# Key products of 64 tokens in two column groups, and waits and placements moved in attention and DeltaNet

## The reference

```
h  = rms_norm(x)*(1+scale)+shift            # scale, shift, gates from silu(c) @ ada_w
p  = h @ w_in                               # q/kv latents, q,k,v of DeltaNet, z, a, b, pooling
attention: 4 heads, softmax(q k^T) v        # latents see all 768 keys, context its own 256
DeltaNet, both directions, 4 heads of 128:  # q, k, v = silu(conv3(.)), q and k normalised
   g = -exp(a_log)*softplus(a+dt), beta = sigmoid(b), gc = cumsum(g) in the chunk
   T = I + strict_lower(beta k k^T * exp(gc_i-gc_j));  w, u = T^-1 (beta k exp(gc)), T^-1 (beta v)
   S <- S exp(gl) + kd^T (u - w S);   o = qg S + (q k^T * decay)(u - w S)
out = [attention, rms_norm(o)*silu(z), pooling] @ w_out;  x += gate1*out
x += gate2*expert_choice_moe(h2)            # 16 experts, top tokens, SwiGLU
```

## Time and profile before

| | us |
|---|---|
| median of 3 runs | 1804.51 (1804.24 to 1807.38) |
| profiled execution | 1800.79 |
| its span, first to last instruction | 1798.7 |
| attention of layer 0, and its DeltaNet tiles | from about 249, from 382 |
| attention of layer 1, and its DeltaNet tiles | from about 1218, from 1308 |
| TensorE's mean granted clock | 0.979 of 2.4 GHz |

### The profile page before, as it was taken

How to read it: one execution, slowest core, us unless ns; L and a number is a source line. 1 busy time by engine, 2 the same in 40 slices (tenths; PEclk the granted TensorE clock), 3 DMA queues, 4 the chain that set the end, 5 groups by cost and what they waited for, 6 DMA issues and landing times. The chain is left out here.

```text
span 1798.7 us, 34350 instructions
## 1 busy us (share of the span) xinstructions
PE 1691.2 (94%) x14201; PEld 1036.1 (58%) x14201; DVE 657.7 (37%) x1330; ACT 448.8 (25%) x991; POOL 414.8 (23%) x556
## 2 busy tenths in 40 slices
PE   6999989879999997999999999999978999999998
PEld 4565555547776554555556445555567844454544
DVE  4045233425554152111211425424446634322323
ACT  4211423252433040011111231143353223001010
POOL 2712105025660003111111141301537700000000
PEclk9999999989999998999999999999989999999999
DMA  9520010067875217999998512000121033699996
GB/s 320 152 87 24 1 37 12 4 196 222 267 248 181 70 64 252 371 369 370 368 357 318 166 47 70 24 1 17 57 82 25 14 117 138 264 411 414 406 413 240
DMA packets 160222, 323.53 MB, mean 180 GB/s; under 512 B 30217, under 2 KB 117999, under 8 KB 144751
## 3 DMA queue, kind: packets, MB, share of 16 engines
q1 hardware_dynamic: 127584, 287.20, 42.8%
q0 software_dynamic: 6880, 21.67, 4.5%
q10 hardware_dynamic: 25646, 13.08, 2.7%
HBM read 307.24 MB, written 14.68 MB: 179 GB/s over the span
## 5 line engine op out<-in xcount | busy, mean ns | idle before, releaser
L676 PE MATMUL psum<-hT,ring 128*128 128x512 f32 (+3 forms) x880 | 298.7, 497 | 0.0
L676 PEld LDWEIGHTS psum<-hT,ring 128*128 128x128 f32 (+1 forms) x880 | 165.6, 190 | 121.3 <-issue 110.9
L1238 PE MATMUL psum<-ring,arena 128*64 128x256 f32 x1536 | 174.4, 384 | 5.6 <-DVE xT L2633 3.4
L1238 PEld LDWEIGHTS psum<-ring,arena 128*64 128x64 f32 x1536 | 109.0, 138 | 68.2 <-issue 13.4
L1138 PE MATMUL psum<-hT,ring 128*128 128x512 f32 (+1 forms) x384 | 139.4, 521 | 0.9 <-DVE xT L2517 0.9
L2604 DVE TENSOR_TENSOR arena<-arena,psum 128x384 f32<-128x384 f32 (+1 forms) x32 | 15.6, 488 | 258.7 <-PE psum L1247 159.5
L1138 PEld LDWEIGHTS psum<-hT,ring 128*128 128x128 f32 x384 | 72.7, 190 | 64.8 <-issue 61.5
L2977 POOL DMA_INDIRECT big<-h_rows_lat,idx x16 | 15.7, 983 | 377.0 <-PE psum L1343 173.7
L2633 DVE SCALAR_TENSOR_TENSOR xT<-psum,modraw,xT 128x512 f32<-128x512 f32 (+1 forms) x136 | 79.7, 621 | 18.7 <-PE psum L1319 12.7
L808 PE MATMUL psum<-hT,ring 128*128 128x256 f32 (+1 forms) x192 | 83.5, 545 | 0.0
L2042 ACT COPY arena<-psum 128x512 f32<-128x512 f32 (+2 forms) x49 | 23.6, 481 | 220.4 <-PE psum L1260 147.2
(11 more groups left out here) (377 smaller groups left out, 3097.0 us busy)
## 6 DMA issues: line engine op xcount, KB each, us to landing
ring<-in_moe_w_gate SPq DMA_DIRECT2D x64, 1024.0 KB, 10.1
ring<-in_ada_w SPq DMA_DIRECT2D x48, 1024.0 KB, 6.8
ring<-in_moe_w_up SPq DMA_DIRECT2D x32, 1024.0 KB, 9.7
hT<-in_moe_w_down SPq DMA_DIRECT2D x24, 1024.0 KB
ring<-in_w_in SPq DMA_DIRECT2D x20, 1024.0 KB, 7.3
big<-in_moe_w_up SPq DMA_DIRECT2D x16, 1024.0 KB, 10.0
sz<-in_moe_w_down SPq DMA_DIRECT2D x16, 1024.0 KB
big<-in_moe_w_down SPq DMA_DIRECT2D x16, 1024.0 KB
```

Source lines behind the costliest of these rows:

```text
L676: m = pe.matmul(b[0:c1 - c0, 0:n], lhsT=w[:, k, c0:c1], rhs=hT[:, k, t0:t0 + n], start=k == 0, stop=k == KD - 1)
L1238: m = pe.matmul(b[e * CAP_L:(e + 1) * CAP_L, 0:2 * P], lhsT=xs[:, k, e, 0:CAP_L], rhs=w[e][:, 2 * (k - ks[0]) + q, :], start=k == 0, stop= ...
```

## The change

The keys' small products become 64 tokens by 64 in two column groups: 16 matmuls to a bank, in three banks, claimed in calls 0, 1 and 2 and not two in call 1. VectorE multiplies each bank (512 columns) by the mask of the diagonal blocks of 16 and sums over the four column blocks with a reduction, behind its copy of the transposes in those calls. ScalarE stores them in call 3, not 2.

The other placements are given for layer 0 and layer 1. The gates' logarithms: call 2 and 1, not 0. The decays from them: call 4 and 2, not 1. The sums over the decays: call 6 and 3, not 2. Their transpose: call 8 and 4, not 3. The lanes' exponentials: call 11 and 7, not 7. Loading the inverse blocks: call 16 and 12, not 21 and 13. The first tile's kk products: one call earlier. The eight SiLUs and both table loads stand ahead of the copy that sets `att`, and `next_decays` of tile 1 in slots 3 and 5 as in the other tiles. In layer 0's first tile the slots have 0, 1, 0, 1, 1, 1, 2 modulation products. `next_decays` waits for the key transposes of tile j - 2 and for decay_state of that tile, and no longer for its state product. GpSimd makes `masks` ahead of `one_sided`, and before tile 0 `spread` ahead of `masks`, in layer 0 ahead of `decays` too.

```diff
-LANES_EXP = 7
+GATES, SUMS, ROWS, LANES_EXP = (2, 1), (6, 3), (8, 4), (11, 7)
+ADA_SLOTS = ((0, 1, 0, 1, 1, 1, 2), (1, 1, 1, 1, 1, 1, 0))
@@ TensorE, block_lanes
-                    if n == 1:
+                    if n in (0, 1, 2):
                         pe.wait_ge(s["lmul"], GH)
-                        for w in range(2):
-                            b = claim(("pk", l, w))
-                            for x in range(NT * GH // 2):
-                                i, h = divmod(w * NT * GH // 2 + x, GH)
-                                for q in range(4):
-                                    t = slice(i * P + 32 * q, i * P + 32 * (q + 1))
-                                    m = pe.matmul(b[32 * q:32 * (q + 1), 32 * x:32 * (x + 1)], lhsT=qkvT[:, GH + h, t],
-                                                  rhs=qkvT[:, GH + h, t], start=True, stop=True)
-                            done(m, ("pk", l, w))
-                    if n == 2:
+                        b = claim(("pk", l, n))
+                        for x in range(2 * GH):
+                            i, h = 2 * n + x // GH, x % GH
+                            for q in range(2):
+                                t = slice(i * P + HALF * q, i * P + HALF * (q + 1))
+                                m = pe.matmul(b[HALF * q:HALF * (q + 1), HALF * x:HALF * (x + 1)], lhsT=qkvT[:, GH + h, t],
+                                              rhs=qkvT[:, GH + h, t], start=True, stop=True)
+                        done(m, ("pk", l, n))
+                    if n == SUMS[l]:
@@ TensorE, first_chunk
-                    if n in (5, 6):
-                        gdn_piece("kk", 0, n - 5)
+                    if n in (4, 5):
+                        gdn_piece("kk", 0, n - 4)
@@ ScalarE, next_decays
                     if j >= 2:
                         act.wait_ge(s["eb"], 2 * (j - 2) + d + 1)
-                        evacuated(act, ("st", l, j - 2, d))
+                        evacuated(act, ("kr", l, j - 2, d))
+                    if j >= 3:
+                        act.wait_ge(s["sdec"], 2 * (j - 3) + d + 1)
@@ ScalarE, gdn_between
-                    if j == 0 and slot < 4:
-                        silu(8 + slot)
-                        gate_silu(slot)
-                    if j == 0 and slot == 3:
-                        act.preload_act_table_set(LOG_EXP)
-                        for d in range(2):
-                            next_decays(1, d)
+                    if j == 0 and slot in G_SLOTS:
+                        next_decays(1, G_SLOTS.index(slot))
@@ ScalarE, first_chunk
-                    if n == 5:
+                    if n == (0, 4)[l]:
                         act.wait_ge(s["xout"], 32 * (l + 1))
                         blocks_back(0)
                         blocks_back(1)
@@ ScalarE, behind the calls
+                act.preload_act_table_set(SILU)
+                for m in range(3):
+                    silu(8 + m)
+                    gate_silu(m)
+                silu(11)
                 gate_out(3)
+                gate_silu(3)
+                act.preload_act_table_set(LOG_EXP)
@@ VectorE
+                def key_blocks(n):
+
+                    if l == 0 and n == 0:
+                        dve.wait_ge(s["scat"], 16)
+                    if n in (0, 1, 2):
+                        b = product_ready(dve, ("pk", l, n)).rearrange("p (x b c) -> p x b c", x=2 * GH, b=4)
+                        x = at(mlaw, n % 2 * 512, (2 * GH, 4, BLOCK))
+                        link(dve.tensor_tensor(x, b, on_diagonal.unsqueeze(1).to_broadcast([P, 2 * GH, 4, BLOCK]), ALU.mult), l)
+                        read_out(dve.tensor_reduce(pairs16[:, 2 * GH * n:2 * GH * (n + 1), :],
+                                                   x.rearrange("p x b c -> p x c b"), AX.X, ALU.add), ("pk", l, n))
+
@@ GpSimd, before tile 0
-                decays(0)
-                masks(0)
                 how = freed_by[lent_prior[l]]
-                product_ready(pool, how[0], how[1])
-                spread(0)
+                if l == 0:
+                    product_ready(pool, how[0], how[1])
+                    spread(0)
+                    decays(0)
+                    masks(0)
+                else:
+                    decays(0)
+                    product_ready(pool, how[0], how[1])
+                    spread(0)
+                    masks(0)
@@ GpSimd, end of a tile
                     if j + 1 < NT:
+                        masks(j + 1)
                         one_sided(j + 1)
-                        masks(j + 1)
```

More of the change, by code:

```diff
@@ L447, in between, with ada_at @@
             return out
+        def ada_at(j, slot):
+            counts = ADA_SLOTS[min(j, 1)]
+            first = ADA_FIRST + ADA_CHUNK * j + sum(counts[:slot])
+            return range(first, first + counts[slot])
         def row_products(l, j):
@@ L938, in gdn_between @@
                     if l == 0:
-                        if slot < ADA_CHUNK:
+                        for a in ada_at(j, slot):
+                            assert a == ada[0]
                             ada_load(0)
                             ada_load(1)
-                        elif j == NT - 1:
+                        if j == NT - 1 and slot == ADA_CHUNK:
                             ada_turn(0)
@@ L1876, in gdn_between @@
                         blocks_back(j + 2)
-                    if l == 0 and slot < ADA_CHUNK:
-                        ada_out(ADA_FIRST + ADA_CHUNK * j + slot)
+                    for a in ada_at(j, slot) if l == 0 else ():
+                        ada_out(a)
                     if l == 0 and j == 4 and slot == 0:
@@ L1942, in _, with gate_silu @@
                         read_out(act.copy(PTs[l][n % 3][1].rearrange("p j c -> p (j c)"), b[:, 0:2 * P]), key)
+                def gate_silu(m):
+                    for g in segs:
+                        evacuated(act, ("in", l, "z%d" % m, g))
+                    act.activation(szT[:, m, t_first:T], szT[:, m, t_first:T], ACT.Silu)
+                act.preload_act_table_set(SILU)
[3 more added lines that the diff above has]
+                silu(11)
                 gate_out(3)
+                gate_silu(3)
+                act.preload_act_table_set(LOG_EXP)
                 for i in tiles:
```

35 lines of the change are left out of this document (11 added, 24 removed).

## The result

The changed kernel takes 1783.55 us (median of 4 runs, 1783.15 to 1786.32) against 1804.9 beside it: a ratio of 0.9882, 95% interval 0.9865 to 0.9900, so 21 us faster. So the pair of traces shows only 14.4 of the 21 us. Single executions of one kernel lie up to 8 us off their median, and the mean granted clock goes with them: of the kernel before, the execution of 1797.96 had 0.983 and the one of 1810.62 had 0.977.

The account below looks back on a forecast made before the run. TensorE, busy in 94% of the span, was taken as the bound, so only its waits and half clock could give time. Terms summed to -23.8 from 1800.79: 1777.0 profiled, 1780.7 median; own range 1768 to 1790, with the first rival to 1797.

Parts of the forecast that it names:

- The signs that I had named: Included hardly any layer 1 factor waits, VectorE subtraction idles of 5 to 7 us, call 17 idle about 3, no spread wait.
- First calls, -1.0: Layer 0's first calls: key products cost +1.1, gates' wait of 1.1 and a third (1.0) go; range -3.7 to +1.5.
- the 2.1 without a name: Part of TensorE's 6.0 us idle in layer 0's first calls that ended on nothing the profile names; kept in the forecast.
- Call 16, +4.6: Layer 0: ScalarE waits 3.1 us for inverse blocks stored late, plus 1.5 for half clock; range 0 to +6.
- Calls 20 to 23, -7.8: Layer 0: -3.5 from the bank wait in call 21, -4.3 from the wait for the spread inverse blocks.
- First tile of layer 0, -4.3: DeltaNet: 15.3 us to be had, 11.0 back, with a 6.6 wait from SiLUs ahead of `att`; range -9 to +2.
- Tiles 1 to 5, -1.5: Layer 0's later DeltaNet tiles: 1.5 of 3.1 us of TensorE idle goes; range -3 to 0.
- Attention, boundary and first tile of layer 1, +0.4 and -3.7: Products +1.1, first wait -1.0, gates 0.3; then 11.3 back of 11.5 wait and 3.5 clock. Ranges -1 to +2, -7 to +1.
- Later tiles of layer 1, -10.5: Waits for masks (5.7) and ScalarE's copies (3.9) go, with 0.9 of clock; range -12.5 to -3.
- later tiles keep their waits: Rival, 15%: decays' DMA or GpSimd's order replaces both waits in layer 1's later tiles; -11.8, giving 1792.7.
- ScalarE becomes the bound: Rival, 7%: block ahead of `att` paid in full, first tiles' waits stay, later tiles give nothing; +11.8, 1816.3.
- more than forecast: Rival, 5%: call 16's wait hidden, unnamed gap goes, first tiles reach lower ends; -37 or below, under 1768.

Follow-up runs that it names:

- a1: Changed kernel with the keys' products as before (32 tokens, four column groups, two banks, call 1): 1784.56 us, ratio 0.9886.
- b4: Kernel before with the new key products alone (64 tokens, two column groups, three banks): 1803.03 us, ratio 0.9990.
- a3: Changed kernel with gates' logarithms, decays, sums, transpose and lanes' exponentials back in the calls of the kernel before: 1782.48 us, ratio 0.9877.
- a2: Changed kernel with the inverse blocks loaded two calls later in layer 0, one later in layer 1: 1781.44 us, ratio 0.9862.
- c3: Changed kernel with the first tile's kk products one call later, as before the change: 1788.25 us, ratio 0.9915.
- c4: Changed kernel with GpSimd's first spread of layer 0 behind decays and masks again, early loads kept: 1784.77 us, ratio 0.9897.
- b3: Changed kernel with the eight SiLUs and both table loads back in the first tile's slots 0 to 3: 1785.70 us, ratio 0.9901.
- b1: Changed kernel with GpSimd's masks behind one_sided again in every tile: 1788.79 us, ratio 0.9918.
- b2: Changed kernel with next_decays waiting for the state product of tile j - 2 again: 1784.55 us, ratio 0.9902.
- a4: Changed kernel with SiLU table load and two SiLUs behind the last exponential, last gate copy ahead of six SiLUs: 1776.22 us, ratio 0.9837.

## Why the prediction was right, and where its steps were not

The forecast was 1780.7 with 1768 to 1797; it came to 1783.55. The sum was -23.8 for medians that moved by 21; the traces moved by 14.4. For the profiled execution I had 1777.0, and it took 1786.32. I had put the median 3.7 above the trace; it came 2.8 below it. So the sum was 9.3 too good in the traces, and part of the small error of the median is luck. The parts below are read from the traces. The signs that I had named came in part: no wait for the spread and 2.2 in call 17, but no idle of 5 to 7 on VectorE's first subtraction in layer 0, and one of 3.0 in layer 1.

**First calls, -1.0; measured -3.4.** The price was near: a group took 1.15 at full clock (1.88 where it ran at half), so 3.45 in all against my 3.0, 36 ns a pass against 31. VectorE's masks took 0.68 and its reductions 1.0, so 5.1 and not 4.1, and they hid: no wait of TensorE names them. What I missed is the gain: I kept the 2.1 without a name, and it belonged to the old products (a1 has it, b4 and a3 don't). What it is stays open: it stands in layer 0 alone, in both kernels that have the 192 small matmuls, and a load of instructions starts ahead of it in both (a1).

```profile
252.57 1.88 PE L1020 MATMUL psum<-big 128*64 128x64 f32 x32 [1.84 <-DVE big L2301]
...
257.32 1.15 PE L1020 MATMUL psum<-big 128*64 128x64 f32 x32
```

```profile
255.45 0.68 DVE L2422 TENSOR_TENSOR mlaw<-psum,lev 128x512 f32<-128x512 f32 x1
256.16 1.00 DVE L2423 TENSOR_REDUCE sz<-mlaw 128x128 f32<-128x512 f32 x1
```

The rule that I weighed there (the Trainium skill, TensorEngine Tiling (Array Packing), Theoretical Speedup) gave by my estimate 1.9 more on TensorE in a layer, the row that I took 1.1; the rows show 1.6, from 1.86 to 3.45, between the two.

**Call 16, +4.6; measured +5.3.** Right in mechanism and size. a2 and a3 show both of its causes, each with 5.3 to 5.4. TensorE's idle grew by 2.2, not 3.1, and the clock behind it cost 3.1, not 1.5.

**Calls 20 to 23, -7.8; measured -8.8**: 7.1 up to t0, and 1.7 from there to the last small products (L861, now L868), where the kernel before was busy at half clock for 3.4 us behind the wait for the spread. Right in size, wrong in one reason of each half. I gave the bank's wait to three banks and to kk together: b4 has three banks and the wait, a1 has two and not, c3 brings it back by kk alone. I gave the spread's wait to its new order and its early loads; c4 shows that the order wasn't needed, and c3 has no such wait with kk late and the new order. So either edit is enough where the loads are early; no run has kk or the order alone with the loads as before.

**First tile of layer 0, -4.3; measured -3.1** (from 6.5 ahead of the last small products to 9.6 at the second tile's factors). The failing step is where the block of SiLUs would be waited for. I had it at VectorE's subtraction, 6.6 long. It came first on TensorE, 2.8, for the bank of the last gate product (L1074), whose copy stood behind seven SiLUs. I had counted that copy's time, not who waits for it. The rest of the block then lay beside the slow matmuls behind that wait: the first level's update (L1006) starts at 382.03 without a wait.

**Tiles 1 to 5, -1.5; measured +0.2.**

**Attention, boundary and first tile of layer 1, +0.4 and -3.7; measured +1.5 and -1.4, nothing together.** In attention TensorE is busy 2.2 longer and idles 0.8 less; exponential 13 came 2.8 later, not 0.7, but TensorE had hardly waited for it, and 1.9 was back by exponential 15. From there on the wait for the spread (2.4) went, and one for the last gate copy (2.5) took its place. With the 3.0 on VectorE's subtraction that makes 5.6, where I had 5.1: the wait right in size, its first half again in another place. The clock was priced too low: it is at half from 1304.0 to 1314.3, with TensorE busy for 7.5 us, and for 3.4 us more at 1321. By the sum's own rule that costs 5.1 in the window of this stage, where I had 2.0. b3 says what that was worth: the block ahead of `att` brings what it costs.

**Later tiles of layer 1, -10.5; measured -7.3.** Both waits were the ones that the releasers named, but the price was too high. The waits for masks fell from 5.7 to 1.7 and those on the last level from 3.9 to 0, yet TensorE's idle fell only from 13.2 to 8.0, since a wait that goes lets the next one grow. The other 2.2 is clock, where I had 0.9, and 1.4 to 1.6 of clock comes and goes there between traces with the same code. b1 gives 3.8 for the masks, 1.4 of it idle (I had 5.7), and b2 1.8 for the decays, all idle (3.9). Left in these tiles are TensorE's waits for VectorE's subtraction, 0.93 in each of two tiles, and for GpSimd's mask (L2859), the longest 1.25.

**The rivals.** Of *later tiles keep their waits* a third was true by the time, and more by the idle (8.0 of 13.2 stayed). *ScalarE becomes the bound* was true in place, not in size: the first tiles gave 3.1 and 1.4. Of *more than forecast* one part in three came: the unnamed gap went. In layer 0 the over- and underpriced terms cancel (-10.0 forecast, -9.6 measured); layer 1 gave 7.3 of 13.8. Between them, in code that the change doesn't touch, 1.8 was lost.

## What to carry to other kernels

Ask of an instruction that is moved not only how long it takes but whose bank, flag or buffer stands behind it in its queue: the block of SiLUs was costed right and its victim was the wrong one. Work for an in-order engine goes into the idle time that it already has (a4: 3.2 us behind the last exponential), and a load of something needed late goes late (a2); these two were worth 13 to 14 us where the whole change was worth 21. And a title names an edit, not the cause: the new products alone moved nothing that can be measured (b4).

## What the runs showed of the hardware

- A product of 64 columns in two column groups took 36 ns a pass at full clock; 32 columns in four groups took 9.7 (1.86 us for 192). Halving the passes cost 1.6 us a layer.
- The sum over four column blocks, 512 elements into 128, took 1.00 to 1.02 us on VectorE, half as much again as the mask over the same 512 (0.68).
- A table load of 1.28 at 369.40 is followed by the next instruction at 370.69, as at the earlier trace rows. Ten of the 15 loads in each trace are followed within 0.02 us, and these two begin within 0.02 us of the end of the instruction ahead: no drain on either side. The rule that I had weighed against the rows (the Trainium skill, ScalarE: Activation LUTs, What ACT_TABLE_LOAD costs) would have put it 1.38 later.
- Over the same 901 matmuls the clock was 0.92 with 10.0 us of idle in one kernel and 1.00 with 11.0 in another, for 2.7 us. That is more than several of the waits removed here, and it isn't settled by them.
